# A 21-stage fp32 network on one core: the projections and output product of the spatial gating stage as three fp32r products, with the lower parts written over the raw weights

## The reference, cut to what matters

```
D_MODEL = 1024; SEQ = 256; SG_CHUNK = 128; SG_WIDTH = 2048; SG_GROUPS = 8

def spatial_gating(h, w_in, ln_g, ln_b, w_s, b_s, w_out):
    B, L, _ = h.shape
    u, v = jnp.split(jax.nn.gelu(h @ w_in), 2, axis=-1)
    v = layer_norm(v, ln_g, ln_b)
    nc = L // SG_CHUNK
    vg = v.reshape(B, nc, SG_CHUNK, SG_GROUPS, SG_WIDTH // SG_GROUPS)
    mixed = jnp.einsum('gts,bcsgd->bctgd', w_s, vg) + b_s.T[None, None, :, :, None]
    return (u * mixed.reshape(B, L, SG_WIDTH)) @ w_out
```

## Time and profile before

| | |
|---|---|
| median of 3 runs | 3731.98 us (3730.28 to 3732.06) |
| the profiled execution, its own time | 3731.42 us |
| its span | 3729.7 us |
| PE busy | 3658.1 us, 98% of the span |
| DVE busy | 2252.2 us, 60% |
| ACT busy | 1474.2 us, 40% |
| POOL busy | 274.2 us, 7% |
| granted PE clock, mean | 0.994 of full speed |
| DMA | 660.51 MB, mean 177 GB/s |

### The profile page before, as it was taken

The page is one execution under the profiler, slowest core; times in us unless marked ns, Lnnn a source line. Parts: engine busy times, 40 slices in busy tenths (PEclk is TensorE's granted clock), DMA queues, the critical chain, the costliest instruction groups (busy, mean ns, idle before and its releaser), DMA issues.

```text
span 3729.7 us, 47536 instructions
## 1 busy us (share of the span) xinstructions
PE 3658.1 (98%) x18606; PEld 3026.4 (81%) x18606; DVE 2252.2 (60%) x2973; ACT 1474.2 (40%) x1957; POOL 274.2 (7%) x322
## 2 busy tenths in 40 slices
PE   8999999999999999999999999999999999999999
PEld 7898788889788875888898688888887688888587
DVE  6767577774577755777776677455434555541254
ACT  4454244443444334444462334444311444431143
POOL 0004200000000000000014000000001100000000
PEclk9999999999999999999999999999999999999999
DMA  9652277673576734766640475646422264553452
GB/s 318 223 159 85 69 245 241 224 233 134 175 259 209 249 133 153 255 224 233 213 150 27 163 251 171 209 136 219 156 93 68 80 207 165 203 197 102 169 182 100
DMA packets 453673, 660.51 MB, mean 177 GB/s; under 512 B 15304, under 2 KB 385443, under 8 KB 453048
## 3 DMA queue, kind: packets, MB, share of 16 engines
q1 hardware_dynamic: 431970, 579.22, 45.7%
q0 software_dynamic: 21072, 78.56, 6.6%
q10 hardware_dynamic: 454, 0.26, 0.0%
HBM read 656.94 MB, written 2.00 MB: 177 GB/s over the span
## 4 chain that ended last, share of the span: by engine, by line
PE 92%; DVE 4%; ACT 2%; issue 1%; ACTq 0%; POOL 0%; POOLq 0%; DVEq 0%
PE ps L806 14%; PE ps L808 14%; PE ps L807 14%; PE ps L826 7%; PE ps L828 7%; PE ps L827 7%; PE ps L1153 4%; PE ps L3110 3%; PE ps L816 2%; PE ps L1573 2%; PE ps L2830 1%; PE ps L2833 1%; DVE parts L743 1%; PE ps L3107 1%; PE ps L1502 1%; PE ps L1488 1%
## 5 line engine op out<-in xcount | busy, mean ns | idle before, releaser
L743 DVE TENSOR_TENSOR parts<-ring,parts 128x2048 fp32r<-128x2048 f32 (+1 forms) x339 | 756.9, 2234 | 612.8 <-ACT parts L729 612.8
L806 PE MATMUL ps<-parts 128*128 128x512 f32 x2288 | 905.3, 396 | 0.5 <-DVE parts L1013 0.3
L808 PE MATMUL ps<-parts 128*128 128x512 f32 x2288 | 891.8, 390 | 0.0
L807 PE MATMUL ps<-parts 128*128 128x512 f32 x2288 | 890.9, 389 | 0.0
L729 ACT ACTIVATE parts<-ring 128x2048 fp32r<-128x2048 f32 x330 | 630.6, 1913 | 574.5 <-PE ps L808 417.3
L808 PEld LDWEIGHTS ps<-parts 128*128 128x128 f32 x2288 | 429.4, 188 | 91.1
L806 PEld LDWEIGHTS ps<-parts 128*128 128x128 f32 x2288 | 429.9, 188 | 86.0 <-issue 1.7
L807 PEld LDWEIGHTS ps<-parts 128*128 128x128 f32 x2288 | 430.2, 188 | 84.8
L826 PE MATMUL ps<-parts 128*128 128x512 f32 x1144 | 450.4, 394 | 0.2
L828 PE MATMUL ps<-parts 128*128 128x512 f32 x1144 | 446.1, 390 | 0.0
L827 PE MATMUL ps<-parts 128*128 128x512 f32 x1144 | 445.3, 389 | 0.0
(11 more groups left out here) (433 smaller groups left out, 4444.0 us busy)
## 6 DMA issues: line engine op xcount, KB each, us to landing
ring<-in_ffn_w_gu SPq DMA_DIRECT2D x176, 1024.0 KB
ring<-in_ffn_w_in SPq DMA_DIRECT2D x110, 1024.0 KB
ring<-in_ffn_w_down SPq DMA_DIRECT2D x88, 1024.0 KB
ring<-in_ffn_w_out SPq DMA_DIRECT2D x55, 1024.0 KB
ring<-in_gdn_w_in SPq DMA_DIRECT2D x32, 1024.0 KB
arena<-in_w_mod POOLq DMA_DIRECT2D x24, 1024.0 KB, 5.8
xn<-in_w_mod POOLq DMA_DIRECT2D x24, 1024.0 KB, 7.4
arena<-in_w_mod POOLq DMA_DIRECT2D x48, 512.0 KB, 9.0
```

What stands on the lines that cost most here:

```text
L743: ins = nc.vector.tensor_tensor(lower, unit_raw(at, j)[:, sides_, :], upper, ALU.subtract)
L806: nc.tensor.matmul(dst, h_u, w_u[:, :, n, :], start=(k == 0), stop=False)
L807: nc.tensor.matmul(dst, h_u, w_l[:, :, n, :], start=False, stop=False)
L808: ins = nc.tensor.matmul(dst, h_l, w_u[:, :, n, :], start=False, stop=(k == KD - 1))
```

## The change

`sgu` becomes a stage with 16 units. Its projections and its output product are made of three fp32r products each; the mixing products stay as they were. The upper parts of the `w_in` units go to the two existing buffers. The lower part of each unit, and of each `w_out` tile, is written by DVE over the raw weights, in the ring slot itself (`ring_parts` is the fp32r view of the same memory). For the output product there are seven buffers of 1024 columns for upper parts, three for the tiles 0 to 2 and four in turn for the rest. h and u are split too, u in place. `sg_u`, `sg_v` and the rows of the layer norm move to other places in `arena`; `sg_lng` moves to `xn`, and its transfer now waits for the turned tokens. Some semaphores are merged.

```diff
-UNITS = {"ffn": NFT, "gdn": 16, "sb": 12}
+UNITS = {"ffn": NFT, "gdn": 16, "sb": 12, "sgu": 16}
...
+        if at["kind"] == "sgu":
+            return gu_hi[:, j % GU_SLOTS, :], part_in_place(unit_load(at, j), j % 3)
         return gu_hi[:, j % GU_SLOTS, :], gu_lo[:, j % GU_SLOTS, :]
+
+    def part_in_place(load, n):
+
+        return ring_parts[load % RING][:, n * PART:(n + 1) * PART]
...
             if n < TT:
-                wait_h(pe, at, n)
+                pe.wait_ge(h_split, NQ * at["split"] + 2 * n + 2)
...
-            if n % 6 == 0:
-                wait_loaded(pe, g)
+            if i == 0:
+                pe.wait_ge(gu_lower, at["unit"] + n // 2 + 1)
             if n >= 4:
                 pe.wait_ge(sgu_s, n - 3)
...
+            w_u, w_l = unit_parts(at, n // 2)
+            if side == "v":
+                ins = row_products(ps[:, n % 4, 0:CH], slice(i * P, (i + 1) * P), w_u, w_l)
+            else:
+                ins = column_products(ps[:, n % 4, 0:T], w_u, w_l, slice(i * P, (i + 1) * P))
...
-        w_out_pe(pe, at, 6, sg_u, tiles=SGT)
+
+        def out_tile(k, q):
...
+            nc.tensor.matmul(dst, u_u, w_u[:, cols], start=first, stop=False, skip_group_check=True)
+            nc.tensor.matmul(dst, u_u, w_l[:, cols], start=False, stop=False, skip_group_check=True)
+            return nc.tensor.matmul(dst, u_l, w_u[:, cols], start=False, stop=last, skip_group_check=True)
+
+        for k in range(SGT - 4):
+            pe.wait_ge(sgu_cen, 2 + 2 * TT + k // 2 + 1)
+            pe.wait_ge(sgu_wl, k + 1)
+            for q in range(NQ):
+                ins = out_tile(k, q)
+                if q == 0 and k and k % 4 == 0:
+                    ins.then_inc(load_used, 1)
+            ins.then_inc(sgu_wd, 1)
+        pe.wait_ge(sgu_wl, SGT)
+        for q in range(NQ):
+            for k in range(SGT - 4, SGT):
+                ins = out_tile(k, q)
...
     def sgu_act(act, at):
...
         for n, (side, q, i) in enumerate(SGU):
-            act.wait_ge(sgu_ps, n + 1)
+            if i == 0 and 0 < n // 2 < UNITS["sgu"] - 1:
+                gu_upper_act(act, at, n // 2 + 1)
+            act.wait_ge(up_done, 2 * at["unit"] + n + 1)
...
-            if n in (20, 24):
-                square((n - 20) // 4)
+            if n in (19, 23):
+                square((n - 19) // 4)
+
+        def w_upper(k):
...
+            if k >= 7:
+                act.wait_ge(sgu_wd, k - 3)
+            nc.scalar.activation(sg_w_upper(k), sg_w_raw(at, k), ACT.Copy).then_inc(sgu_wu, 1)
...
+        for k in range(3):
+            w_upper(k)
+        for n in range(SGG):
+            act.wait_ge(sgu_y, n + 1)
+            nc.scalar.activation(sg_u_parts(2 * n, 2)[0], sg_u(2 * n, 2), ACT.Copy).then_inc(sgu_ss, 1)
+        for k in range(3, SGT):
+            w_upper(k)
...
     def sgu_dve(dve, at):
...
+        for j in range(1, UNITS["sgu"]):
+            if j + 1 < UNITS["sgu"]:
+                gu_lower_dve(dve, at, j + 1)
+            if j == 8:
...
+                mean(0)
+            if j == 9:
+                center(0)
+                mean(1)
+            if j == 10:
+                center(1)
+            if j == 12:
+                scale(0)
+            if j == 13:
+                shift(0)
+            if j == 14:
+                scale(1)
+            if j == 15:
+                shift(1)
...
+        for n in range(SGG):
+            if n < 3:
+                w_lower(n)
+            gate(n)
+            if n:
+                u_lower(n - 1)
+        u_lower(SGG - 1)
+        for k in range(3, SGT):
+            w_lower(k)
         add_to_x(dve, at, w_out_done(dve, at), x_sb, 1.0, gate_row)
```

More of the change, by code:

```diff
@@ L164, in build @@
     both = parts("parts", [P, PARTS])
+    ring_parts = [parts(f"ring_parts{i}", [P, SLOT]) for i in range(RING)]
     class Pieces:
@@ L190, in build @@
     xn = sb("xn", [P, TT, D])
-    ring = sb("ring", [P, RING, SLOT])
     x_sb = sb("x_sb", [P, TT, D])
@@ L397, in splits_alone @@
     def splits_alone(at):
-        return at["kind"] in UNITS and not (at["kind"] == "ffn" and at["n"] >= 8)
+        return at["kind"] in UNITS and not (at["kind"] == "sgu" or at["kind"] == "ffn" and at["n"] >= 8)
     def h_before(at):
@@ L2765, in build, with sg_u_parts, sg_w_upper, sg_w_raw @@
     car = Carve()
-    sg_v = car.take(TT, SGW)
-    sg_lng = car.take(SGW)
+    sg_u2 = car.take(SGT // 2, T)
+    car.take(T + GU_SLOTS * GU, 1)
     sg_lnb = car.take(SGW)
     sg_ws = car.take(SGG, P)
-    sg_wsT = car.take(SGG, P)
-    sg_bs = car.take(SGG, P)
-    sg_u = car.take(SGT, T)
+    sg_bs = car.take(SGG, P)
+    sg_v = car.take(TT, SGW)
+    sg_u1 = car.take(SGT // 2, T)
+    assert car.at == H_LO
+    car.take(KD * T, 1)
+    sg_wsT = car.take(SGG, P)
+    sg_lng = xn[:, :, :].rearrange("p t d -> p (t d)")
+    SG_W = [2304 + GU_SLOTS * GU + n * D for n in range(3)] + [2304 + 2 * GU_SLOTS * GU + n * D for n in range(4)]
+    def sg_u_parts(c, n=1):
+        half, at_ = divmod(c, SGT // 2)
+        upper = (h_hi, h_lo)[half]
+        lower = both[:, TT * D + (H_LO - KD * T, 0)[half]:][:, 0:KD * T].rearrange("p (a b) -> p a b", b=T)
+        return upper[:, at_:at_ + n, :], lower[:, at_:at_ + n, :]
+    def sg_w_upper(k):
+        a = TT * D + SG_W[k if k < 3 else 3 + k % 4]
+        return both[:, a:a + D]
+    def sg_w_raw(at, k):
+        return ring[:, (at["load"] + 6 + k // 4) % RING, (k % 4) * D:(k % 4 + 1) * D]
+    def sg_w_lower(at, k):
+        return ring_parts[(at["load"] + 6 + k // 4) % RING][:, (k % 4) * D:(k % 4 + 1) * D]
+    def sg_u(c, n=1):
+        half = sg_u1 if c < SGT // 2 else sg_u2
+        return half[:, c % (SGT // 2):c % (SGT // 2) + n, :]
     sg_mean = sb("sg_mean", [P, 6])
     sgu_loaded = sem("sgu_loaded")
-    sgu_ps = sem("sgu_ps")
+    sgu_wu = sem("sgu_wu")
+    sgu_wl = sem("sgu_wl")
+    sgu_wd = sem("sgu_wd")
     sgu_s = sem("sgu_s")
@@ L2821, in sgu_pe @@
                     ins.then_inc(sgu_mix, 1)
[L2822 to L2824 removed]
+            if i == 0:
+                pe.wait_ge(gu_lower, at["unit"] + n // 2 + 1)
             if n >= 4:
                 pe.wait_ge(sgu_s, n - 3)
[L2827 to L2835 removed]
+            w_u, w_l = unit_parts(at, n // 2)
[3 more added lines that the diff above has]
+                ins = column_products(ps[:, n % 4, 0:T], w_u, w_l, slice(i * P, (i + 1) * P))
+            ins.then_inc(up_done, 1)
         pe.wait_ge(sgu_cen, 2 + 2 * TT)
@@ L2892, in sgu_dve, with scale @@
-        for t in range(TT):
+        def scale(t):
             v = sg_v[:, t, :]
+            dve.wait_ge(sgu_loaded, 64)
             dve.wait_ge(sgu_rs, t + 2)
```

93 lines of the change are left out of this document (62 added, 31 removed).

## The result

The changed kernel takes 3707.02 us, the median of 4 runs (3705.92 to 3711.59); the kernel before, run beside it, 3731.13 us (3726.90 to 3732.06). The ratio is 0.9939, with a 95% interval of 0.9924 to 0.9955. The forecast was 3712.0 with a range of 3706.5 to 3717.5, so the time lies in the range, near its lower end. The profiled execution took 3707.07 us, with a span of 3705.4.

What follows compares the result with a forecast made beforehand. PE was taken as the bound, with 92% of the time. Savings of 29.8 us less waits and a clock fall gave −20.0 us: 3711.4 on the profiled execution's scale, 3712.0 on the median's, range 3706.5 to 3717.5.

Steps and rivals of the forecast that it cites:

- The products: PE in `sgu`: three split products replace each fp32 product, −18.3 us in the projections and −11.5 in the output product, −29.8 together.
- The start: First groups of both token halves in `sgu`: PE waits bare for the lower parts of h, +1.7 us each.
- The squares: Sums of squares on ACT ahead of an upper part: PE waits before units 11 and 13, +2.0 us.
- The mixing: Mixing products: DVE's extra lower parts stay hidden, output product starts 15.0 us after the mixing as now, 0 us.
- The gap ahead of tile 12: Output product: PE waits for all four last tiles, tile 15's split chain behind tile 11 being bare, +2.7 us.
- The clock after it: Behind tile 12's gap: clock falls to half speed for some 3.3 us, half of it lost, +1.65 us.
- The end: Next turning ready about 11.4 us after PE's restart: +0.5 us without the clock's fall, nothing with it.
- the 0.1 ahead of it: `ffn` 11's last block: half a lower part lands ahead of the first add, +0.1 us.
- The waits were not covered: Rival: squares and both starts cost nothing, only the output product's gap stays; 3702 to 3707 us, chance 0.13.
- the second rival: More waits in the stage, or the clock falls at the start too; 3715 to 3722 us, chance 0.17.
- The pace of an fp32 pass: Rival: a split product costs one of an fp32 product's four passes, 0.215 or 0.108 us; about 3700 us, chance 0.02.
- The slower rival: Split becomes the bound: its 4.75 us chain is bare in each of 14 units; +50 us, about 3762, chance 0.03.

Runs made afterwards that it cites:

- e9_all: Changed kernel with four edits together: squares moved, start drawn apart, seven upper buffers for w_out's tiles, adds first; median 3704.59 us, stage 159.64 us.
- e7c_start: Changed kernel, group 0 starting on four blocks of h, units 0 and 1 on the first token half first, unit 2 with its own buffer; stage 165.00 us.
- e6_squares: Changed kernel with ACT's two sums of squares moved behind an upper part; median 3706.93 us, stage 165.46 us.
- e4c_buffers: Changed kernel with seven upper buffers for w_out's tiles to the end, and DVE's first `ffn` 12 lower parts waiting for tile 11; stage 165.92 us.
- e5c_adds_first: The kernel of e4c_buffers with the adds of quarters 0 and 1 ahead of the first lower part of `ffn` 12; stage 165.65 us.
- e0: Changed kernel run once more, no edit; stage 168.33 us, beginning at 3335.33.
- e8c_one_buffer: Changed kernel with the next unit's upper part issued behind both gelus of a unit, as with one upper buffer; 3803.97 us, stage 261.45 us.
- e11: Changed kernel a third time, no edit, on the chip of the second run of the four-edit kernel; six executions between 3703.81 and 3714.33 us.
- e2_proj_only: Changed kernel with the output product as one fp32 product again, on raw weights and raw u; median 3718.51 us, stage 175.4 us.

## Why the prediction was right, and where it was off

**The products, −29.8.** Right. From the wait at 3424.90 to the mixing at 3442.28 lie six groups in 17.38 us, 17.28 by 2.88 each and 0.1. From the first output product to tile 12 it is 3492.59 − 3457.28 = 35.31 us, which is 12 × 2.72 and the gap. e9_all shows the second pace without a gap: 43.78 us for 192 products is 192 × 0.2267 = 43.5 and some 0.25. That the lower parts are read from the ring's memory changes no pace.

**The start, +1.7 and +1.7.** Right: 3342.58 − 3336.90 = 5.68 us for 5.6, and 3349.99 − 3345.55 = 4.44 for 4.4, from the turning to the group. Against the earlier trace rows these are 1.77 and 1.71 us more; e7c_start takes 2.50 of them back.

**The squares, +2.0.** Right, 2.04 by e6_squares, at the two units named.

**The mixing, 0.** Right: 3457.28 − 3442.28 = 15.00 us.

**The gap ahead of tile 12, +2.7.** Right: 35.31 − 32.64 = 2.67; e4c_buffers takes it away with the buffers.

**The clock after it, +1.65.** Right for the profiled execution, and a little large. A fall takes 1.49 us of PE's time: 121.87 − 120.38 in e5c_adds_first, and 12.63 − 11.14 at the end of the changed kernel against the unhindered end of e5c_adds_first. The forecast called a fall somewhat likelier than not; 2 of the 6 profiled executions with a gap of 2.40 or 2.41 us had one (the changed kernel, e0), 4 did not (e6, e7, e8, e11).

**The end.** Right in kind, a little small. Without the fall the turning comes at 11.81 us after the restart where 11.4 was forecast, with it at 12.63 where 12.5 was. The fall's net cost is therefore 0.82 us, and not 1.1. The rest of its 1.49 us hides behind DVE's adds, which bound the end when PE runs at full clock: PE waits 0.63 us for DVE ahead of the turning in e6_squares and nowhere in e5c_adds_first, where the adds come first.

**The sum.** −20.0 forecast for the stage and the 0.1 ahead of it, −19.86 measured in the stage with the fall and 167.50 − 188.18 = −20.68 without (−21.1 forecast). The 0.1 us ahead of the stage can't be told from the falls there.

**The time, 5.0 us under the forecast.** No step of the sum failed. The prediction was made against one execution, with 22.1 us of clock lost ahead of the stage, and the four runs of the changed kernel lay on its good side. Over 15 runs its mean is 3708.9, which is 20.65 less than the 58 of before, with a standard error of 0.9. So the sum is borne out, but that the median of four stayed inside the range, by 0.5 us, is in part luck: 5 of those 15 executions took less than 3706.5. What the prediction lacked is a term of its own in the range for the falls elsewhere, which move single executions of the kernel before by up to 11 us.

**The rivals.** The waits were not covered: the time lies at the edge of that rival's range, 3702 to 3707, for another reason, and e6, e7 and e4 each show the wait that it denied. A fall of the clock at the start, the second rival, did occur in one execution of a near copy (e5c_adds_first) and cost 1.5 us, near its 1.7. The pace of an fp32 pass is excluded by 0.120 and 0.2267. The slower rival's mechanism is real, and its price was wrong. It was put at 50 us; e8c_one_buffer takes 261.45 − 188.18 = 73 us more in the stage than the kernel before, because 14 waits bring 14 stretches at 1.2 GHz, some 28 us, that the rival did not count. Its time of 3762 is also a slip of the sum: the 50 us count from a unit of 6.9 us in the kernel before, but are added to the forecast of 3712, whose units take 5.76. From there it is 14 × 4.75 = 66.5 us less the 2.0 of the squares, some 3776; e8c_one_buffer took 3803.97 (two executions), 28 us more.

## What to carry to other kernels

An operand split is hidden by the lead that its buffers allow, so for each place where PE needs all of several parts at once (the last four tiles), or where something longer stands ahead of an upper part (the squares), count how far ahead the copy may start; here these places, two bare starts and a fall of the clock behind one of the gaps gave back 9.9 us of 29.8, and order and buffers alone recovered 8.7 (7.9 against an execution without the fall). Where work for the next stage stands ahead of this stage's last adds, ask which of the two PE needs first. Measure an edit of 1 to 5 us by the time between two marks inside a trace, where it repeats to 0.02 us: medians of five or six runs of one and the same kernel differed by 5 to 6 us (3706.18 and 3711.22; 3704.59 and 3698.84), and in e2_proj_only the median would have picked the wrong theory.

## What was not expected

- The changed kernel loses between 15.4 and 23.9 us of TensorE's clock ahead of `sgu`, in falls of about 1.7 us each. Some come in every trace, others in one execution and not in the next.
- A gap of 2.4 us at identical work on both sides was followed by a fall in 2 of 6 executions, one of 1.9 us (group 0 in the changed kernel, e0, e2, e4, e5, e6, e8 and e11) in 1 of 8, the waits of e8c_one_buffer in 14 of 14. No length between 1.9 and 2.4 us decides alone: gaps of 2.40 or 2.41 us had no fall behind them four times, and one of 1.91 us had one.
- A wait that repeats is dearer than its length: 14 waits of 4.6 us cost 6.9 us each.
